# Gate products of a recurrent block cut to the columns they need, and a second buffer for the gate weights

## What is computed

```python
D_RNN = 5 * D_MODEL // 4          # 2560
N_GATE_BLOCKS = 16
GATE_BLOCK = D_RNN // N_GATE_BLOCKS   # 160
...
xr = causal_depthwise_conv(proj[..., D_RNN:], conv_w, conv_b)
xb = xr.reshape(B, L, N_GATE_BLOCKS, GATE_BLOCK)
r = sigmoid(einsum('blnc,ncd->blnd', xb, w_r).reshape(B, L, D_RNN) + b_r)
i = sigmoid(einsum('blnc,ncd->blnd', xb, w_i).reshape(B, L, D_RNN) + b_i)
```

## Time and profile before

| | |
|---|---|
| three runs | 3256.79, 3256.52, 3251.93 us; median 3256.52 |
| profiled execution | 3252.73 us, its span 3250.9 us |
| mean granted TensorE clock | 0.997 of full speed |
| busy share of the span | PE 98%, PEld 95%, DVE 58%, ACT 46%, POOL 6% |
| chain that ended last | PE 87%, DVE 6%, ACT 3%, DMA 2% |

### The profile page before, as it was taken

One profiled execution on the slowest core, in us unless ns is written; L12 is line 12 of the kernel. 1 busy time (PEld: TensorE's weight loads), 2 busy tenths in 40 slices (PEclk: granted clock), 3 DMA queues, 4 the chain that ended last, 5 costly groups with the idle time before them and its releaser, 6 DMA issues.

```text
span 3250.9 us, 59566 instructions
## 1 busy us (share of the span) xinstructions
PE 3198.9 (98%) x25789; PEld 3101.3 (95%) x25789; DVE 1891.5 (58%) x1696; ACT 1509.4 (46%) x1596; POOL 183.9 (6%) x164
## 2 busy tenths in 40 slices
PE   8999999999999999999999999999999999999998
PEld 8998889999789999999999999999988999999998
DVE  7755554767777655554544445555776555545454
ACT  5455553656556754443433334433454434434343
POOL 1140000000021200000000000100001000000001
PEclk9999999999999999999999999999999999999999
DMA  7564443899764455555655555555434666666664
GB/s 252 157 189 136 143 133 123 279 291 302 269 223 150 137 169 173 177 175 176 179 181 173 177 181 179 179 169 180 149 124 143 194 194 194 194 192 193 192 194 147
DMA packets 552496, 598.39 MB, mean 184 GB/s; under 512 B 9920, under 2 KB 531136, under 8 KB 552320
## 3 DMA queue, kind: packets, MB, share of 16 engines
q1 hardware_dynamic: 550416, 589.18, 57.6%
q0 software_dynamic: 1760, 6.59, 0.7%
q10 hardware_dynamic: 144, 0.01, 0.0%
HBM read 593.64 MB, written 2.10 MB: 183 GB/s over the span
## 4 chain that ended last, share of the span: by engine, by line
PE 87%; DVE 6%; ACT 3%; DMA 2%; issue 1%; SPq 0%; POOL 0%; DVEq 0%; ACTq 0%; POOLq 0%
PE acc L621 24%; PE acc L626 23%; PE acc L624 23%; DVE low L1926 2%; PE psx L1186 1%; PE acc L1088 1%; PE acc L1090 1%; PE acc L1089 1%; ACT high L1342 1%; DMA raw<-in_w_expert_gate 1%; PE acc L1171 1%; PE psx L1171 1%; PE acc L1169 1%; PE psx L1169 1%; PE psx L1170 1%
## 5 line engine op out<-in xcount | busy, mean ns | idle before, releaser
L621 PE MATMUL acc<-gh,high 128*128 128x256 f32 (+1 forms) x4416 | 899.5, 285 | 5.6 <-DVE low L1926 3.9
L624 PE MATMUL acc<-gl,high 128*128 128x256 f32 (+1 forms) x4416 | 885.8, 282 | 0.0
L626 PE MATMUL acc<-gh,low 128*128 128x256 f32 (+1 forms) x4416 | 885.8, 282 | 0.0
L2213 DVE TENSOR_TENSOR low<-raw,high 128x2048 fp32r<-128x2048 f32 x264 | 605.1, 2292 | 399.7 <-ACT high L1578 399.7
L1926 DVE TENSOR_TENSOR low<-raw,high 128x2048 fp32r<-128x2048 f32 x261 | 606.2, 2326 | 331.9 <-ACT high L1342 331.4
L1578 ACT ACTIVATE high<-raw 128x2048 fp32r<-128x2048 f32 x264 | 505.4, 1914 | 494.4 <-DMA raw<-in_mlp_w 486.8
L621 PEld LDWEIGHTS acc<-gh,high 128*128 128x128 f32 x4416 | 680.6, 188 | 17.4 <-issue 8.4
L626 PEld LDWEIGHTS acc<-gh,low 128*128 128x128 f32 x4416 | 678.5, 189 | 0.0
L624 PEld LDWEIGHTS acc<-gl,high 128*128 128x128 f32 x4416 | 676.4, 188 | 0.0
L1342 ACT ACTIVATE high<-raw 128x2048 fp32r<-128x2048 f32 x261 | 498.6, 1913 | 315.6 <-DMA raw<-in_w_kv 67.9
L621 PE MATMUL acc<-fh,high 128*128 128x272 f32 (+1 forms) x2048 | 408.9, 281 | 0.0
(11 more groups left out here) (471 smaller groups left out, 3587.3 us busy)
## 6 DMA issues: line engine op xcount, KB each, us to landing
raw<-in_mlp_w SPq DMA_DIRECT2D x256, 1024.0 KB, 5.4
raw<-in_w_in SPq DMA_DIRECT2D x59, 1024.0 KB, 5.3
raw<-in_a_w_in SPq DMA_DIRECT2D x40, 1024.0 KB, 5.0
raw<-in_w_expert_up SPq DMA_DIRECT2D x32, 1024.0 KB, 5.9
raw<-in_w_expert_down SPq DMA_DIRECT2D x32, 1024.0 KB, 5.2
raw<-in_w_kv SPq DMA_DIRECT2D x32, 1024.0 KB, 5.5
raw<-in_w_expert_gate SPq DMA_DIRECT2D x28, 1024.0 KB, 5.7
raw<-in_a_w_out SPq DMA_DIRECT2D x20, 1024.0 KB, 5.0
```

The lines of the kernel that those rows point to most:

```text
L621: pe.matmul(o[n], hw[:, k, c[n]], h, start=first and not (packed and n), stop=False, skip_group_check=packed)
L624: pe.matmul(o[n], hw[:, k, c[n]], l, start=False, stop=False, skip_group_check=packed)
L626: m = pe.matmul(o[n], lw[:, k, c[n]], h, start=False, stop=last, skip_group_check=packed)
L2213: dve.tensor_tensor(tile(low, k, k % SLOTS), tile(raw, k, k % SLOTS), tile(high, k, k % SLOTS).bitcast(F32), ALU.subtract)\
```

## The change

It has two parts.

**Narrow products.** For output tile b the own row tile b keeps its product of 128 columns, now first. Of each neighbour only the columns are multiplied in which it has weights: `side_pieces` cuts the 128 columns in pieces of 128, 64 or 32, aligned to their size, each with the one neighbour that it needs.

| b | products for a gate before | products for a gate now (columns of weights, from column) |
|---|---|---|
| 0 | 128, 128 | 128; 128 from 0 |
| 1 | 128, 128, 128 | 128; 32 from 0, 32 from 32, 64 from 64 |
| 2 | 128, 128, 128 | 128; 64 from 0, 64 from 64 |
| 3 | 128, 128, 128 | 128; 64 from 0, 32 from 64, 32 from 96 |
| 4 | 128, 128 | 128; 128 from 0 |

**Two buffers.** `band_even` holds groups 0 and 2, `band_odd` groups 1 and 3. `band_even` lies where the early part of `rh3` will stand later. SP issues the loads of the four groups before units 8, 11, 15 and 20 (before: 8, 15, 20, 25). Group 1 waits only for POOL's second clearing, groups 2 and 3 for the end of groups 0 and 1. POOL clears two tiles instead of one. For want of a free semaphore, `odd_band_in` is one that was used once at the start.

```diff
+def side_pieces(b):
+    of = [[a for a in range(SUP) if a != b and P * a < RBLK * (m + 1) and P * a + P > RBLK * m]
+          for m in ((P * b + 32 * g) // RBLK for g in range(4))]
+    out, g = [], 0
+    while g < 4:
+        n = next(n for n in (4, 2, 1) if g % n == 0 and all(of[g + x] == of[g] for x in range(n)))
+        out.append((of[g][0], 32 * g, 32 * n))
+        g += n
+    return out
+SIDES = [side_pieces(b) for b in range(SUP)]
...
-        band, w = at("band", [P, 2, BAND_W], w)
+        band_odd, w = at("band_odd", [P, 2, BAND_W], w)
+        band_even, _ = at("band_even", [P, 2, BAND_W], HID + 2 * 2 * (TB + CONV))
+        bands = (band_even, band_odd)
...
+        odd_band_in, ODD0 = x_in[3], 16
...
-                g = {8: 0, 15: 1, 20: 2, 25: 3}.get(u)
+                g = {8: 0, 11: 1, 15: 2, 20: 3}.get(u)
                 if g is not None:
-                    if g:
-                        sp.wait_ge(rg_mm, SUP * g)
+                    if g >= 2:
+                        sp.wait_ge(rg_mm, SUP * (g - 1))
                     else:
-                        sp.wait_ge(band_clear, 1)
+                        sp.wait_ge(band_clear, g + 1)
...
-                        sp.dma_start(band[r0 - P * a:r1 - P * a, :, c:c + RBLK],
+                        sp.dma_start(bands[g % 2][r0 - P * a:r1 - P * a, :, c:c + RBLK],
...
-                            .then_inc(band_in, 16)
+                            .then_inc(odd_band_in if g % 2 else band_in, 16)
...
                 if b == 0:
-                    pe.wait_ge(band_in, 16 * len(BPIECES) * (g + 1))
+                    if g % 2:
+                        pe.wait_ge(odd_band_in, ODD0 + 16 * len(BPIECES) * (g // 2 + 1))
+                    else:
+                        pe.wait_ge(band_in, 16 * len(BPIECES) * (g // 2 + 1))
...
-                meets = [a for a in range(SUP) if BC[a] <= P * b < BC[a] + BWID[a]]
                 for j in range(2):
-                    for a in meets:
-                        c = BOFF[a] + P * b - BC[a]
-                        m = pe.matmul(psx[:, 2 * j + t % 2, 0:TB], band[:, j, c:c + P], xr[:, SUP * g + a, :],
-                                      start=a == meets[0], stop=a == meets[-1])
+                    for a, at_, n in [(b, 0, P)] + SIDES[b]:
+                        c = BOFF[a] + P * b - BC[a] + at_
+                        m = pe.matmul(psx[at_:at_ + n, 2 * j + t % 2, 0:TB], bands[g % 2][:, j, c:c + n], xr[:, SUP * g + a, :],
+                                      start=a == b, stop=a != b)
...
-            pool.memset(band[:, :, :], 0.0).then_inc(band_clear, 1)
+            for g in range(2):
+                pool.memset(bands[g][:, :, :], 0.0).then_inc(band_clear, 1)
```

## The result

The changed kernel takes 3259.43 us, the median of 20 runs (3255.18 to 3263.26). The kernel before, run beside it on the same chip, takes 3254.88 (20 runs, 3250.22 to 3258.34). The ratio is 1.0015, with a 95% interval of 1.0009 to 1.0021: 4.6 us slower. That lies within the 0.2% that the prediction called no difference, but the interval leaves 1 out. The profiled execution takes 3258.22 us.

The account below looks back on a forecast made before the run. PE was taken to bound the kernel; narrow products +7.0 us and the second buffer -3.2 sum to +3.8, giving 3260.3 us against the median, range 3249 to 3265: no difference that can be told.

Parts of the forecast that it names:

- Full tiles and b = 2: Gate products on PE: b = 0 and 4 unchanged; b = 2 from 1.374 to 1.266 us a gate, -0.11.
- b = 1 and 3: Gate products on PE with 32- and 64-column pieces: 1.864 us a gate, +0.49; all narrow products together +7.0 us.
- one width after the other with a stop: PE strips: 64 and 32 columns do not overlap, and each change between them stops PE 0.14 us; chance 0.62.
- the first rival: Strips of 64 and 32 columns run side by side on PE: -5.8 us in all, 3250.7 us; chance 0.25.
- the second: Narrow pieces do not run side by side on PE at all: +14.8 us in all, 3271.3 us; chance 0.08.
- The second buffer: Gate-weight loads go out earlier, removing PE's stops ahead of the first gates of groups 1 to 3: -3.2 us.
- nothing is left of the stops: PE's load waits before groups 1 to 3, together 3.2 us, vanish since each load is over 30 us early.
- PE waits for no sigmoid here: In the gate stage, ACT's sigmoids shift by under a microsecond and hold up no PE product.
- unit 11's: On SP, unit 11's load goes out 5.1 us later behind the eight gate-weight loads; cover 10.8 us, cost 0.

Follow-up runs that it names:

- equal widths: Changed kernel with the 64-column pieces of b = 1 and 3 cut into two of 32; 3246.86 us, ratio 0.9976 to the kernel before.
- two buffers: Kernel before plus the two buffers alone, all gate products still 128 columns wide; 3252.62 us, ratio 0.9998 to the kernel before.
- both gates together: 32-column pieces for b = 1 and 3, plus own-tile products of both gates first, then both gates' strips, against changed kernel; 3246.12 us, ratio 0.9975 to before.
- unit's load first: Changed kernel with SP issuing the unit's load ahead of the eight gate-weight loads, the only edit; 3256.75 us, ratio 1.0011 to the kernel before.

## Why the prediction was right, and where it was not

The forecast of +3.8 us and 3260.3 stands beside +4.6 and 3259.43. That 3260.3 comes out so near has luck in it: it was counted from the first three runs of the kernel before (3256.52), which lie 1.6 above the median of all 20 (3254.88), and the change was put 0.8 too low. The terms, one by one:

- *Full tiles and b = 2.* A gate of b = 2 was to cost 1.266 us; the tile takes 2.53 = 2 x 1.265. Right.
- *b = 1 and 3.* 1.864 for a gate was expected, 3.68/2 = 1.84 measured; three changes of width cost 1.84 - 3 x 0.458 = 0.47, not 0.49. From the 32 columns to the 64 it was to be about 0.6 us, and is 0.59; from tile 1 to tile 2 9.7, and is 9.67. The assumption on which the term rested, one width after the other with a stop, held, and the first rival (8.5 us from tile to tile) and the second (10.6) did not come about. As a whole +6.6 for +7.0.
- *The second buffer.* The 3.2 us of stops are gone, as reckoned. SP issues group 1's loads at 982.41, forecast 983.1; PE waits for no load, POOL's second clearing hides itself, and unit 11's later load makes no stop.
- *The step that failed* is "nothing is left of the stops" with "PE waits for no sigmoid here". The text asked what the moved loads push back, and found unit 11's, with 10.8 us of cover. It did not ask about the loads that take the place that group 1's had: eight loads, now group 2's, still stand ahead of unit 15's. In the kernel before they delayed ACT just as much: ACT waited 10.68 us for that load, and the sigmoid of tile 4 ended at 1033.84:

```profile
1029.75 1.91 ACT L1342 ACTIVATE high<-raw 128x2048 fp32r<-128x2048 f32 x1 [10.68 <-DMA raw<-in_a_w_in]
...
1033.36 0.48 ACT L1740 ACTIVATE rr<-psx,aux 128x272 f32<-128x272 f32 x1
...
1034.29 0.62 PE L1186 MATMUL psx<-xr,band 128*128 128x272 f32 x2
```

PE wanted it at 1034.29, 0.45 us later, and so showed no wait. It came that late only because it had stopped 1.51 us at tile 5. Without that stop it would want the sigmoid at 1032.78, about 1.1 us before it ends; in the changed kernel PE begins another 0.2 us after the sigmoid's end (1034.69 to 1034.92), so some 1.3 us, an estimate, were to be expected and 1.4 came. Nearly half of the 3.2 us of stops had moved, not gone: the second buffer was worth 1.8, not 3.2. The rows for this were all in the trace of before. The 1.4 us less the 0.4 by which the narrow products were cheaper is the 1.0 us by which the stage's +4.8 exceeds +3.8.

## What to carry to other kernels

When a stop is taken away, go on along the same queue and see which waits the stop had been hiding: whatever was ready less than its length ahead of time is late next. In this kernel narrow products paid only where neighbours had equal widths, and most where the change of width was paid rarely: cutting the wide piece into more instructions of the narrow width, and gathering the strips of both gates, turned their +6.6 us into -6.8. On an in-order queue, look which load is needed first: here eight small loads ahead of a large one cost 1.4 us, and behind it nothing.

## What the runs showed beside this

Four 32-column products of a tile, 16 narrow passes for both gates, add up in sums that a full product has just begun, and cost no more than four full passes and the two changes of width. Before these runs no row showed strips doing so side by side.

In the profile of the equal widths the stop at tile 6 is 1.9 us long, and behind it the granted clock falls. Stretches behind that stop (columns as above):

```profile
1034.20:1035.40 1.20, 1.20 (x11) 0.41 (x11) 1.20 (x3) 1.18 (x3) 0.60 (x1) 1.00 1.01 340
1037.00:1038.00 1.00, 1.00 (x7) 0.67 (x4) 0.93 (x3) 0.98 (x3) 0.00 (x0) 0.50 0.01 5
...
1040.00:1042.00 2.00, 2.00 (x18) 2.00 (x18) 1.37 (x3) 2.00 (x2) 0.89 (x1) 1.00 0.00 0
```

PE had waited 1.9 us and then run full and narrow products for some 1.5 us at 1.00 (2.4 GHz); from about 1035.6 on it was granted 0.50 (1.2 GHz), and from 1039.1 on 1.00 again. With stops of 1.4 us (changed kernel), 1.5 (two buffers) and 1.7 (both gates together) the clock stays at 1.00 in this stage.

The length of a stop does not settle it. Late in the program, in code that the change does not touch, PE stops for 2.9 us in every one of the eight profiles, for the same operation of ACT. Within 1.5 us of that stop's end the clock fell in four of them (before, equal widths, both gates, unit's load first) and stayed at 1.00 in the other four. The kernel before, with the stop ahead of 2441.29 us, and the changed kernel, with the stop ahead of 2444.91:

```profile
2442.80:2446.20 3.40, 3.40 (x13) 2.47 (x13) 2.97 (x3) 1.52 (x2) 0.00 (x0) 0.50 0.00 0
...
2445.00:2449.00 4.00, 4.00 (x27) 3.51 (x28) 2.31 (x2) 2.94 (x2) 0.00 (x0) 1.00 0.00 0
```

So a fall like that at tile 6 may belong to the one execution that was profiled and not to the kernel. What decides it was not tried.
